# One block for the first projection, the state-space chunks and the head norm, with the units in the order u, v, q, k

## The chip, the cores and the metric

The kernel runs on one NeuronCore of one Trainium2 chip. The metric is the device time of one execution in microseconds; three runs of the kernel before took 4768.56, 4768.86 and 4769.66 us, median 4768.86. The execution that the profiler recorded took 4769.85 us, of which its span from the first to the last instruction is 4768.1 us. In what follows PE is TensorE, DVE is VectorE, ACT is ScalarE, POOL is GpSimd and SP is the queue that issues most DMAs.

## The reference, cut to what matters

The program is one block with attention, a state-space mixer, memory attention and a large expert layer, and then two more layers. Only the opening of the first block is touched:

```python
proj = _rmsnorm(h, norm_mix_g[l]) @ w_in[l]          # 512 tokens, 1024 -> 2048
q = proj[..., :512]; k = proj[..., 512:1024]          # 8 heads of 64 each
v = proj[..., 1024:1536]; u = proj[..., 1536:]
att = _chunked_attention(_rmsnorm(q, att_q_g), _rmsnorm(k, att_k_g), v, rel_bias)
ssm = _s5_mixer(u, ...)

def _s5_mixer(u, ...):                                # 32 groups of 16 channels, 64 complex states
    bu_r = einsum('blgc,gpc->blgp', uf, bbr); bu_i = einsum('blgc,gpc->blgp', uf, bbi)
    _, _, xr, xi = associative_scan(_complex_affine_combine, (a_r, a_i, bu_r, bu_i), axis=1)
    y = einsum('blgp,gcp->blgc', xr, c_re) - einsum('blgp,gcp->blgc', xi, c_im) + d_skip * uf
    ...                                               # gelu, gate, both untouched
```

## The kernel before, in words

**The projection** is one call of `project` (line 496, called at L2217). Weights come in 16 pages of 128x1024 through a ring of seven slots. ACT rounds each weight page to its high part (L190), POOL subtracts that to get the low part (L196), and PE multiplies three times for each pair of tiles: low weights by high activations, high by low, high by high. A "features" unit is one PSUM bank with 24 matmuls over 512 columns (L442, L443, L444); a "tokens" part fills four banks side by side, 12 matmuls for each of eight steps over the contraction (L616, L618, L619), so none of its four banks is complete before the end of the part. The units before are u (0 to 3), q (4 to 7), k (8 to 11) and v (the tokens part, 12 to 15). They rotate over six banks: unit n may start only after DVE has scaled unit n-6 out of its bank (semaphore `free`, L581 and L611). DVE does so at L2197 for u, at L2162 for q and k, at L2169 for v.

**The tables.** Between two such evacuations DVE works through a generator, `turn_tables` (L307, passed as `beside`), for a budget of 5.2 us by its own cost figures ahead of each features unit and 3.5 times that ahead of the first tokens unit. It makes powers of the state's decay, then 17 sets of three instructions over 128x512 (L390, L393, L396): eight for the matrices that lead into a state (`into`), nine for those that lead out of it (`outof`), then cosines and sines by doubling, and last a copy of the decay to 64 chunks (`rate`, L430). Whatever is left of the generator is run after the last budget.

**The chunks.** `state_chunks` (L1548) treats the 512 tokens as 64 chunks of 8. In a block of its own PE transposes the 32 matrices of `into` (L1595, ACT copies them out of PSUM), multiplies them with u read back through DRAM by chunks (`enter`, L1608, four batches of eight groups), and DVE turns each batch and scans it over the chunks (L1692 to L1698). The effect inside a chunk goes through eight lag kernels: 32 matmuls of 16 columns for all groups (L1652), an ACT copy, four transposes (L1659) and a spreading by DVE (L1716). Then for each batch: a matmul that swaps real and imaginary halves (`swap_ends`, L1617), DVE turns the states back (`leave`, L1707 to L1710), PE multiplies them with `outof` (L1627), ACT copies the result (L1682) and SP writes it to DRAM and reads it back in another order (L1577 to L1586), and PE adds the lags (`inside`, L1638). DVE closes each quarter with L1736.

**The head norm** (`head_norm`, L775, called at L2223) is a third block: ACT squares q and k (L802), PE sums them (L816), ACT and DVE take the root, PE spreads it (L830), DVE scales q and k (L861). After it a fourth block starts the attention.

Each `nc.Block()` ends when all engines have come to its end; the next one starts them together. Inside a block each engine runs its instructions in program order and waits on semaphores only.

## Time and profile before

| | us |
|---|---|
| median of three runs | 4768.86 |
| profiled execution | 4769.85 |
| its span | 4768.1 |
| PE busy in the span | 4498.3 (94%) |
| DVE / POOL / ACT busy | 2004.3 / 1842.5 / 1461.5 |
| first matmul of the projection | 12.72 |
| last matmul of the projection | 121.5 |
| first transpose of the chunks | 129.51 |
| last matmul of the chunks | 196.5 |
| first matmul of the head norm | 203.82 |
| first matmul of the attention | 227.75 |

The last six rows are times from the start of the span. The share of PE's busy time is an average over the whole program; what the touched stretch costs is read from its own part of the timeline. "PEclk" in a row is the share of full speed (2.4 GHz) that TensorE was granted; 0.50 is 1.2 GHz.

### The profile page before, as it was taken

To read this page: it belongs to the slowest core of one execution; us is meant where nothing else is said; L and a number is where in the kernel's file an instruction comes from. 1 tells how busy PE (TensorE), PEld (TensorE's weight loads), DVE (VectorE), ACT (ScalarE), POOL (GpSimd) and SP (SyncE) were. 2 spreads that over 40 slices of the span, in tenths; PEclk is the share of its full clock that TensorE was granted. 3 is DMA by queue.
4 is the path that set the end of the run, shared out by engine and by line. 5 is a ranking of instruction groups with operands and counts; after the bars stand their busy time and mean duration, and the time that the engine had idled before them with its cause. 6 is when DMAs were issued, how large, how long until landed. Compare 5 with 4: busy or idle time off the path is not lost. (4 is left out here: it accounts for less than half of the span.)

```text
span 4768.1 us, 51289 instructions
## 1 busy us (share of the span) xinstructions
PE 4498.3 (94%) x19930; PEld 3524.0 (74%) x19930; DVE 2004.3 (42%) x4177; ACT 1461.5 (31%) x2188; POOL 1842.5 (39%) x828
## 2 busy tenths in 40 slices
PE   7778899999999999999999979899999998788999
PEld 6557578888888888887887836588878874365887
DVE  8463369933332333333441252444144135645440
ACT  2153323344443111112222235432232232344221
POOL 3015144466665444444444401244444431032443
PEclk9789999999999999999999989999999999999999
DMA  3213134455555655654222201222222221021222
GB/s 139 45 50 111 44 102 135 139 166 177 172 183 190 196 186 184 197 184 148 93 97 94 97 16 36 67 91 95 97 89 97 95 85 51 18 76 49 97 94 83
DMA packets 220707, 520.43 MB, mean 109 GB/s; under 512 B 25649, under 2 KB 91569, under 8 KB 217521
## 3 DMA queue, kind: packets, MB, share of 16 engines
q1 hardware_dynamic: 135984, 450.03, 28.9%
q10 hardware_dynamic: 84480, 67.12, 4.3%
q8 instruction: 159, 2.61, 0.2%
q14 instruction: 84, 0.68, 0.0%
HBM read 445.77 MB, written 71.30 MB: 108 GB/s over the span
## 5 line engine op out<-in xcount | busy, mean ns | idle before, releaser
L196 POOL TENSOR_TENSOR ring_rounded<-ring,highs_rounded 128x1024 fp32r<-128x1024 f32 x687 | 1681.2, 2449 | 2644.2 <-ACT highs_rounded L190 2644.2
L442 PE MATMUL bank<-arena_rounded,ring_rounded 128*128 128x512 f32 (+1 forms) x4488 | 1778.9, 396 | 85.1 <-DVE hT_rounded L460 41.5
L444 PE MATMUL bank<-arena_rounded,highs_rounded 128*128 128x512 f32 (+1 forms) x4488 | 1757.9, 392 | 0.0
L190 ACT ACTIVATE highs_rounded<-ring 128x1024 fp32r<-128x1024 f32 x687 | 728.1, 1061 | 2039.1 <-PE bank L444 1598.5
L443 PE MATMUL bank<-hT_rounded,highs_rounded 128*128 128x512 f32 x3128 | 1221.6, 391 | 0.0
L442 PEld LDWEIGHTS bank<-arena_rounded,ring_rounded 128*128 128x128 f32 x4488 | 853.8, 190 | 271.4 <-issue 82.5
L444 PEld LDWEIGHTS bank<-arena_rounded,highs_rounded 128*128 128x128 f32 x4488 | 850.6, 190 | 193.9
L443 PE MATMUL bank<-arena_rounded,highs_rounded 128*128 128x512 f32 (+1 forms) x2112 | 824.3, 390 | 0.0
L443 PEld LDWEIGHTS bank<-hT_rounded,highs_rounded 128*128 128x128 f32 x3128 | 592.6, 189 | 125.3 <-issue 0.2
L443 PEld LDWEIGHTS bank<-arena_rounded,highs_rounded 128*128 128x128 f32 x2112 | 402.4, 191 | 86.4
L1526 DVE TENSOR_TENSOR arena<-qT,arena 128x512 f32<-128x512 f32 x64 | 149.9, 2342 | 363.6 <-ACT qT L1491 363.0
L2080 DVE TENSOR_SCALAR arena<-mats,arena 128x128 f32<-128x128 f32 x512 | 156.7, 418 | 336.8 <-PE bank L1889 336.7
L1972 ACT ACTIVATE arena<-bank 128x512 f32<-128x512 f32 x128 | 76.6, 598 | 471.5 <-PE bank L444 471.5
L438 DVE CAST arena_rounded<-arena 128x512 fp32r<-128x512 f32 x128 | 54.6, 427 | 386.6 <-PE bank L444 386.6
L442 PE MATMUL bank<-qT_rounded,ring_rounded 128*128 128x512 f32 x512 | 203.5, 397 | 0.0
L1533 DVE SCALAR_TENSOR_TENSOR xT<-bank,xT 128x512 f32<-128x512 f32 x32 | 22.1, 692 | 427.8 <-PE bank L444 427.5
L444 PE MATMUL bank<-qT_rounded,highs_rounded 128*128 128x512 f32 x512 | 200.9, 392 | 0.0
L2094 DVE TENSOR_TENSOR arena<-arena 128x512 f32<-128x512 f32 x128 | 105.8, 826 | 137.6 <-DMA arena<-gate_table 133.2
L1940 ACT ACTIVATE qT<-bank 128x512 f32<-128x512 f32 x128 | 135.0, 1138 | 22.9 <-PE bank L1889 22.9
L1889 PEld LDWEIGHTS bank<-arena 128*128 128x128 f32 x1024 | 126.0, 191 | 6.1
L1889 PE MATMUL bank<-arena 128*128 128x128 f32 x1024 | 126.4, 275 | 0.0
L1526 DVE TENSOR_TENSOR arena<-kT,arena 128x512 f32<-128x512 f32 x24 | 59.0, 2458 | 153.9 <-ACT kT L1491 153.9
(351 smaller groups left out, 4172.8 us busy)
## 6 DMA issues: line engine op xcount, KB each, us to landing
ring<-pages_in SPq DMA_DIRECT2D x687, 512.0 KB, 3.4
act_table<-arena SPq DMA_DIRECT2D x128, 256.0 KB, 4.0
gate_table<-qT SPq DMA_DIRECT2D x16, 2048.0 KB, 7.2
arena<-act_table ACTq DMA_DIRECT2D x128, 256.0 KB, 3.9
arena<-gate_table ACTq DMA_DIRECT2D x32, 1024.0 KB, 8.0
arena<-mem_in SPq DMA_DIRECT2D x3, 1024.0 KB, 5.1
arena<-spread_in SPq DMA_DIRECT2D x5, 512.0 KB, 4.4
xT<-x_in SPq DMA_DIRECT2D x8, 256.0 KB, 6.2
```

Source lines behind the costliest of these rows:

```text
L190: nc.scalar.activation(f32r(page_high(p)), slot(p), ACT.Copy).then_inc(masked_pages.sem, 1)
L196: nc.gpsimd.tensor_tensor(f32r(slot(p)), slot(p), part_of(page_high(p)), ALU.subtract).then_inc(split_pages.sem, 1)
L438: return nc.vector.tensor_copy(f32r(out), x)
L442: low_last = nc.tensor.matmul(out, f32r(w_low), f32r(x_high), start=start, stop=False)
L443: nc.tensor.matmul(out, f32r(w_high), f32r(x_low), start=False, stop=False)
L444: return low_last, nc.tensor.matmul(out, f32r(w_high), f32r(x_high), start=False, stop=stop)
L1526: nc.vector.tensor_tensor(w_low(f), w_high(f), up_scaled, ALU.mult).then_inc(made2.sem, 1)
L1889: last = nc.tensor.matmul(bank[4 + b][:, k * P:k * P + P], one1[:, b, k, :], one2[:, b, k, :], start=True, stop=True)
L1940: nc.scalar.activation(wide[:, h % 2, :, k * quad:k * quad + quad].rearrange("p j t -> p t j"), bank[4 + q % 4][:].rearrange("p (t j) -> p ...
L1972: nc.scalar.activation(kept[:, r % 2, :], bank[r % 2][:], ACT.Gelu).then_inc(made.sem, 1)
L2080: last = nc.vector.tensor_scalar(one1[:, b, k, :], iota, turnedT[:, 1, t:t + 1], turnedT[:, 0, t:t + 1], ALU.is_equal, ALU.mult)
L2094: nc.vector.tensor_tensor(raw[:, r % 3, :].rearrange("p (h t) -> p h t", h=n_half), acts_in[:, b, :].rearrange("p (h t) -> p h t", h=n_hal ...
```

## The change

1. The three blocks become one: `project`, `state_chunks` and `head_norm` take a block from outside, so that the barriers at their ends go, and waits on semaphores stand in their place.
2. The pages are laid out and the units run in the order u, v, q, k.
3. The part of u for the groups 0 to 23 is read back by chunks after weight page 15 has been asked for, into a place of its own; the part for the groups 24 to 31 after weight page 22, as the whole was before.
4. The 32 matmuls of 16 columns (L1652) are gone. The input matrices of lag 0 (`first_in`, one more set of three in the tables) are put beside the states as 16 further columns, so that the matmuls that lead out of the states take 80 columns instead of 64 and give the lag kernels too. `outof` now has eight powers (0 to 7), not nine, and `into` and `in_re` one power more each.
5. Of the sets for `outof` five stay in the tables and three are made at the start of the chunks; the copy of the decay is made for each batch.
6. The four transposes of the lags come one by one after each batch's `leave`, and `inside` runs one batch later.
7. In the chunks the banks are numbered anew (entering into 0 to 3, transposes and leaving in 4 and 5). PE's part of the head norm waits until DVE has closed the four quarters (`made2`), and the last quarter of the outputs is read back after the load of `spread`.

The diff, cut to its core:

```diff
@@ turn_tables
-            yield from turn(in_re, in_im, power_re[:, 0:8, :], power_im[:, 0:8, :], over(fr, 8), over(fi, 8), 8, groups)
+            yield from turn(in_re, in_im, power_re[:, 1:9, :], power_im[:, 1:9, :], over(fr, 8), over(fi, 8), 8, groups)
+            link(nc.vector.tensor_scalar(minus_fi, fi, gcol("sign"), -1.0, ALU.mult, ALU.mult))
...
-            for first, other, by_first, by_other, out, order in (
-                    (raw_b, other_b, in_re, in_im, into, [(7 - j, j) for j in range(8)]),
-                    (raw_c, other_c, power_re, power_im, outof, [(l, l) for l in range(9)])):
...
+            for l in range(8):
+                yield from three(raw_b, other_b, banked[0][:, l, :], banked[1][:, l, :], into[:, :, 7 - l, :])
+            yield from three(raw_b, other_b, fr, minus_fi, first_in)
             link.eng.sem_inc(tables_made.sem, 1)
...
+            for l in range(late_powers):
+                yield from three(raw_c, other_c, banked[0][:, l, :], banked[1][:, l, :], outof[:, :, l, :])
...
-            link(nc.vector.tensor_copy(rate, mag8[:, :, None].broadcast_to([P, groups, n_chunks])))
-            link(nc.vector.memset(rate[:, :, 0:1], 0.0))
-            yield 3.5
@@ state_chunks, PE
-                        if q >= 2:
-                            pe.wait_ge(turned2.sem, turned2.at(q - 1))
+                    if q < 2:
+                        pe.wait_ge(free.sem, free.at(q - 5))
+                    else:
+                        pe.wait_ge(turned2.sem, turned2.at(q - 1))
...
+                    if b >= 2:
+                        pe.wait_ge(shifted.sem, shifted.at(b - 1))
+                    else:
+                        pe.wait_ge(free.sem, free.at(2 * b - 2))
...
-                            last = nc.tensor.matmul(bank[0][:, n_chunks * g:n_chunks * g + n_chunks],
-                                                    outof[:, batch * b + g, 1:9, :].rearrange("p l c -> p (l c)"),
-                                                    before[:, batch * b + g, :], start=True, stop=True)
+                        at = wide * (g % 4)
+                        last = nc.tensor.matmul(bank[4 + g // 4][:, at:at + wide],
+                                                outof[:, batch * b + g].rearrange("p l c -> p (l c)"),
+                                                before[:, batch * b + g, :], start=True, stop=True)
...
-                    for g in range(groups):
-                        last = nc.tensor.matmul(bank[0][:, 16 * g:16 * g + 16],
-                                                outof[:, g, 0:8, :].rearrange("p l c -> p (l c)"), into[:, g, 7, :],
-                                                start=True, stop=True)
-                    last.then_inc(compared.sem, 1)
...
                     for b in range(batches):
                         leave(b)
                         if b + 2 < batches:
                             swap_ends(b + 2)
-                        inside(b)
+                    turn_lags(b)
+                    if b >= 1:
+                        inside(b - 1)
+                inside(batches - 1)
@@ state_chunks, ACT
+                    for j in range(2):
+                        last = nc.scalar.activation(
+                            lags[:, P * b + 64 * j:P * b + 64 * j + 64].rearrange("p (g c) -> p g c", g=4),
+                            left[j][:, :, n_chunks:wide], ACT.Copy)
+                    last.then_inc(drawn.sem, 1)
@@ state_chunks, DVE
+                for l in range(late_powers, chunk):
+                    link(nc.vector.tensor_tensor(q0, raw_c, over(power_re[:, l, :]), ALU.mult))
+                    link(nc.vector.tensor_tensor(q1, other_c, over(power_im[:, l, :]), ALU.mult))
+                    link(nc.vector.tensor_tensor(outof[:, :, l, :], q0, q1, ALU.add))
@@ calls
-        project(H, MH, DC, SEQ, [("features", 4, times_by_chunks), ("features", 4, times(Q)), ("features", 4, times(K)),
-                                 ("tokens", TB, times_token(lambda t: V4[:, t, :]))],
...
+        with nc.Block() as first_mixer:
+            project(H, MH, DC, SEQ, [("features", 4, times_by_chunks), ("tokens", TB, times_token(lambda t: V4[:, t, :])),
+                                     ("features", 4, times(Q)), ("features", 4, times(K))],
...
+            state_chunks(U, first_mixer)
```

Where the tokens part starts, PE's order changes as follows (L616, L618, L619 before are L623, L625, L626 after; L499 spreads the norm's root). First before, behind the last unit of k:

```order
290 L442 MATMUL bank5<-arena_rounded_54,ring_rounded_49 128x512
291 L443 MATMUL bank5<-hT_rounded_51,highs_rounded_50 128x512
292 L444 MATMUL bank5<-arena_rounded_54,highs_rounded_50 128x512
293 L616 MATMUL bank0<-ring_rounded_49,arena_rounded_54 128x512 [waits free,split_pages]
294 L618 MATMUL bank0<-highs_rounded_50,hT_rounded_51 128x512
295 L619 MATMUL bank0<-highs_rounded_50,arena_rounded_54 128x512
296 L616 MATMUL bank1<-ring_rounded_49,arena_rounded_54 128x512 [waits free]
```

And now, behind the last unit of u:

```order
99 L499 MATMUL bank6<-mats,params 128x128 [waits inverted]
100 L499 MATMUL bank6<-mats,params 128x128 x3
101 L623 MATMUL bank4<-ring_rounded_49,arena_rounded_54 128x512 [waits split_pages]
102 L625 MATMUL bank4<-highs_rounded_50,hT_rounded_51 128x512
103 L626 MATMUL bank4<-highs_rounded_50,arena_rounded_54 128x512
104 L623 MATMUL bank5<-ring_rounded_49,arena_rounded_54 128x512
105 L625 MATMUL bank5<-highs_rounded_50,hT_rounded_51 128x512
106 L626 MATMUL bank5<-highs_rounded_50,arena_rounded_54 128x512
107 L623 MATMUL bank0<-ring_rounded_49,arena_rounded_54 128x512 [waits free]
```

The part moved ahead by eight units; two of its banks are empty anyway, and the wait on `free` is now for the first and second unit of u, not for the third to sixth bank of q and k.

On PE behind the last matmul of the projection, first before (L1595 transposes, L1608 enters, L1652 makes the lags):

```order
389 L533 UNCONDITIONAL_BRANCH
390 L1588 UNCONDITIONAL_BRANCH [waits barrier_Pool_Activation_PE_DVE_SP_release]
391 L1595 MATMUL bank<-mats,arena 128x128 x8
...
410 L1608 MATMUL bank<-qT,hT 128x64 [waits shifted,turned2]
411 L1608 MATMUL bank<-qT,hT 128x64 x15
412 L1652 MATMUL bank<-arena 128x16 [waits turned2]
413 L1652 MATMUL bank<-arena 128x16 x31
414 L1617 MATMUL bank<-arena,params 128x512 [waits exped]
```

And now (L1609 transposes, L1627 enters, L1636 swaps, L1648 leaves, L1657 transposes the lags, L1665 is `inside`):

```order
389 L1600 UNCONDITIONAL_BRANCH
390 L1609 MATMUL bank<-mats,arena 128x128 [waits free]
391 L1609 MATMUL bank<-mats,arena 128x128 x3
...
413 L1627 MATMUL bank<-qT,hT 128x64 x15
414 L1636 MATMUL bank<-hT,params 128x512 [waits exped]
415 L1636 MATMUL bank<-arena,params 128x512 [waits exped]
416 L1648 MATMUL bank<-arena 128x80 [waits turned2,weighed]
417 L1648 MATMUL bank<-arena 128x80 x7
418 L1636 MATMUL bank<-arena,params 128x512 [waits weighed,exped]
419 L1657 MATMUL bank<-mats,small 128x128 [waits shifted,drawn]
```

The wait on the barrier has gone, and the matmuls of 16 columns no longer stand between entering and leaving.

On DVE, behind the tables, the order now is (L2199 evacuates k, L1759 to L1761 are the late sets, L1721 and L1723 the decay of a batch, L1725 its first instruction):

```order
222 L339 TENSOR_TENSOR qT<-bank,arena 128x16x32
223 L2199 TENSOR_TENSOR kT<-bank,small 128x512 [waits full,dve_step]
224 L2199 TENSOR_TENSOR kT<-bank,small 128x512 [waits full]
225 L1714 UNCONDITIONAL_BRANCH
226 L1759 TENSOR_TENSOR arena<-qT,arena 128x512 [waits groups_in]
...
234 L1761 TENSOR_TENSOR arena<-arena 128x32x16 [waits dve_step]
235 L1721 COPY hT<-arena 128x512 [waits dve_step]
236 L1723 MEMSET hT 128x8 [waits dve_step]
237 L1725 TENSOR_TENSOR arena<-bank,qT 128x512 [waits scored,dve_step]
```

Nine instructions over 128x512 now stand between the last evacuation and the first batch, and the table steps end before the last two units of k.

## Rows read from the trace of the kernel before

**Rows 1.** Windows by stage: us; busy PE, PEld, DVE, ACT, POOL; PEclk; DMA.
```profile
42.30:86.30 44.00, 44.00 (x195) 36.09 (x194) 42.08 (x64) 10.11 (x11) 21.59 (x9) 1.00 0.31 108
86.30:121.50 35.20, 25.16 (x97) 19.10 (x95) 31.94 (x94) 4.07 (x4) 9.90 (x4) 0.85 0.18 61
121.50:129.50 8.00, 0.02 (x1) 0.02 (x1) 7.39 (x11) 0.00 (x0) 0.00 (x0) 0.82 1.21 154
129.50:157.30 27.80, 26.42 (x161) 25.53 (x161) 9.79 (x12) 6.90 (x16) 0.00 (x0) 0.68 0.18 13
157.30:171.50 14.20, 14.20 (x74) 12.42 (x73) 5.56 (x10) 0.60 (x1) 0.00 (x0) 0.64 0.00 1
171.50:196.60 25.10, 25.02 (x133) 18.62 (x132) 12.94 (x17) 2.39 (x4) 0.00 (x0) 1.00 0.24 69
196.60:203.80 7.20, 0.00 (x0) 0.00 (x0) 2.16 (x4) 1.95 (x3) 0.00 (x0) 0.85 0.35 87
203.80:213.30 9.50, 9.44 (x16) 1.62 (x16) 0.00 (x0) 4.26 (x7) 0.00 (x0) 0.75 0.10 31
```

**Rows 2.** Timeline of PE where the tokens part waits: start, us, instruction, idle before.
```profile
99.56 0.80 PE L616 MATMUL bank<-ring_rounded,arena_rounded 128*128 128x512 f32 x1 [4.00 <-DVE kT L2162]
```

**Rows 3.** Timeline of DVE in the projection.
```profile
44.67 1.10 DVE L2197 TENSOR_TENSOR kT<-bank,small 128x512 f32<-128x512 f32 x1
50.47 1.10 DVE L2197 TENSOR_TENSOR kT<-bank,small 128x512 f32<-128x512 f32 x1
...
87.81 2.71 DVE L393 TENSOR_TENSOR arena<-qT,arena 128x512 f32<-128x512 f32 x1
90.55 0.69 DVE L396 TENSOR_TENSOR arena<-bank,arena 128x512 f32<-128x512 f32 x1
...
125.02 1.23 DVE L430 COPY arena<-arena 128x2048 f32<-128x2048 f32 x1
...
126.46 2.73 DVE L2169 TENSOR_SCALAR arena<-bank,params 128x512 f32<-128x512 f32 x4
```

**Rows 4.** Timeline of POOL at that moment.
```profile
87.26 2.71 POOL L196 TENSOR_TENSOR ring_rounded<-ring,highs_rounded 128x1024 fp32r<-128x1024 f32 x1 [3.08 <-ACT highs_rounded L190]
```

**Rows 5.** Timeline of PE in the state-space chunks.
```profile
129.51 4.01 PE L1595 MATMUL bank<-mats,arena 128*128 128x128 f32 x16 [8.00 <-PEq L533]
...
141.50 6.93 PE L1608 MATMUL bank<-qT,arena 128*128 128x64 f32 x32
...
149.93 7.50 PE L1608 MATMUL bank<-qT,hT 128*128 128x64 f32 x64
157.27 10.66 PE L1652 MATMUL bank<-arena 128*128 128x16 f32 x64
...
171.56 1.89 PE L1627 MATMUL bank<-arena 128*128 128x64 f32 x16
...
174.21 4.10 PE L1638 MATMUL bank<-kT,arena 128*128 128x512 f32 x16
```

**Rows 6.** Timeline of DVE in the chunks.
```profile
159.85 1.22 DVE L1698 TENSOR_TENSOR_SCAN hT<-arena 128x512 f32<-128x512 f32 x1
168.03 0.09 DVE L1727 MEMSET arena<- 128x32 f32 x1 [6.96 <-PE bank L1652]
...
170.66 0.68 DVE L1710 TENSOR_TENSOR arena<-arena 128x504 f32<-128x504 f32 x1
...
196.56 0.75 DVE L1736 SCALAR_TENSOR_TENSOR kT<-kT,col,bank 128x512 f32<-128x512 f32 x1 [5.04 <-PE bank L1638]
```

**Rows 7.** PE alone in windows of one us: length, busy, clock.
```profile
133.00:134.00 1.00, 0.52 (x3) 0.81 0.09 6
137.00:138.00 1.00, 1.00 (x7) 0.50 0.00 0
150.00:151.00 1.00, 1.00 (x9) 0.78 0.00 0
```

**Rows 8.** Timeline of SP's queue at the end of the chunks.
```profile
193.62 7.81 SPq L1577 DMA_DIRECT2D qT<-y_table  x16
```

More of the change, by code:

```diff
@@ L398, in turn_tables, with by_channel, three @@
-            link.eng.sem_inc(tables_made.sem, 1)
+            def by_channel(x):
+                return x[:, :, None].broadcast_to([P, groups, 16])
+            def three(first, other, by_first, by_other, out):
+                link(nc.vector.tensor_tensor(a, first, by_channel(by_first), ALU.mult))
+                yield cost(512)
+                link(nc.vector.tensor_tensor(b, other, by_channel(by_other), ALU.mult))
+                yield cost(512)
+                link(nc.vector.tensor_tensor(out, a, b, ALU.add))
+                yield cost(512)
@@ L531, in blocks @@
                     start += c
-            with nc.Block() as block:
+            with (nc.Block() if within is None else nullcontext(within)) as block:
                 @block.sync
@@ L2227, in build @@
+        for b in range(4):
+            y_kept[b].close(16)
         keep = lambda c: hT[:, c, :]
```

364 lines of the change are left out of this document (187 added, 177 removed).

## The prediction, before the change was run

> **What bounds the kernel now.** I read the page's busy shares first (PE 94% of the span), then the windows by stage, then the timelines of PE, DVE, ACT and SP in the touched stretch, and last the clock in windows of one us. The reader is to see in the windows [rows 1] that PE sets the time in all stages here, by its work or by what it waits for: it is busy throughout from 42.3 to 86.3, then 25.16 of 35.2 us while v is projected, not at all in the 8.0 us behind it, 26.42 of 27.8 us in the entering matmuls, all of the next 39.3 us, and not at all in the 7.2 us ahead of the head norm. Nothing behind the head norm is touched, and the attention waits for a block's start, so whatever the head norm's end gains or loses arrives at the end of the program. I therefore follow one chain: the projection's last matmul (121.5), the entering, the leaving, the head norm's first matmul (203.8).
>
> **1. Units in the order u, v, q, k: -4.6 us.** A features unit takes 44.0 / 8 = 5.5 us, and the 96 matmuls of the tokens part would take as much as four units, 22.0 us [rows 1]. Before they took 35.2: PE waited 10.0 us until DVE, which the tables hold up, had emptied the banks of k (the second wait is the 4.00 us of [rows 2]), and at half clock after each wait it lost the other 3.2. Now the part starts at 42.3. Its first two tiles go to banks 4 and 5, which are empty (1.4 us, to 43.7). The third needs the first unit of u gone from bank 0; DVE does that from 44.67 to 45.8 [rows 3], so PE waits 2.1. It takes 0.7, and the fourth needs the second unit, which goes at 50.47 to 51.6 [rows 3]: 5.0 us more. A restart at half clock I price at 1.5 us, half of the 3.2 that two cost before (between nothing and 3.2). Lost: 8.6 instead of 13.2. The last eight units find their banks free: DVE empties v after the large budget, at 82, and q's units at about 88, 94, 99 and 105, while the reuse by k comes at 95 to 117. So PE ends the projection at 42.3 + 22.0 + 8.6 + 44.0 = 116.9.
>
> DVE must be ready too. Its tables and evacuations run without a gap to 129.2 [rows 3]. Taken out of the projection are the set of the ninth power, 4.2 us with its long instruction (0.73, then 87.81 to 91.24), two further sets net (three late, one new) at 3 x 0.73 = 2.2 each, and the copy of the decay with its memset, 1.4; added is 0.2 for `minus_fi`: 129.2 - 4.2 - 4.4 - 1.4 + 0.2 = 119.4. That is 2.5 us behind PE. It is hidden: PE begins with transposes (4.0 us) into banks emptied earlier, and only the second batch of entering needs the last bank of k.
>
> **2. No barrier behind the projection: -8.0 us** [rows 1]. Before, PE waited for DVE's remaining tables and v's evacuation. The two bounds: the whole 8.0, or 5.5 if the 2.5 us of DVE's lag came to stand on the path. I take 8.0.
>
> **3. Transposes and entering: -1.3 us.** The 27.8 us [rows 1] had 1.4 of idle time, nearly all a wait for u read back through DRAM. Three quarters of u are now asked for after weight page 15, about 79, and have landed long before. The last quarter is asked for once weight page 15 is used up (117) and is wanted some 20 us later. Work stays the same: 16 + 32 transposes and 128 entering passes. Their price hangs on the clock: the second batch took 6.93 us at half clock, the third and fourth together 7.50 at full [rows 5, 7]. I keep the mixture of before. All at full, PE saves 6.93 - 3.75 = 3.2 and another 1.5 in the first batch, but then DVE is the bound (below); all at half costs 2 x 3.2 + 1.7 = 8 more. Entering ends at 116.9 + 26.5 = 143.4.
>
> DVE ahead of its first batch has nine instructions (6.5 us): 119.4 + 6.5 = 125.9, then the decay (1.23 / 4 + 0.15 = 0.5). PE's first batch ends at 116.9 + 4.0 + about 5 = 126. They meet, with no slack to speak of; the following batches cost DVE 3.6 + 0.5 = 4.1 us against PE's 8, so DVE catches up again. DVE's earliest end of all four is 125.9 + 4 x 4.1 = 142.3.
>
> **4. From entering to leaving: -7.0 us.** Before, PE's first leaving matmul came at 171.56, 14.3 us behind the last entering one: the lags' matmuls of 16 columns (10.66 us) stood between, and DVE sat idle 6.96 us for them [rows 5, 6]. Now DVE alone is the path: the last batch (159.85 + 1.22 - 157.27 = 3.8), its decay 0.5, the copy of `first_in` 0.7 (a 512-element instruction), the memset 0.1, and three of 0.72 = 2.2 [rows 6]: 7.3. Leaving starts at 150.7.
>
> **5. The four batches: +5.1 us.** Before they took 25.1 us at full clock [rows 1]: leaving 1.89 and lags 4.10 [rows 5] four times, two swaps. Added are: four transposes of a quarter us each (4.01 / 16), 1.0; the ACT copy between leaving and transposing (2.39 / 4 = 0.6, with its hand-overs 0.7), covered by a swap in the first two batches and open in the last two, 1.4; 80 columns instead of 64. For these the bounds are nothing (16 columns took no less each than 64 at either clock, [rows 5], so loading weights is the limit) and a quarter of 1.89 each; I take 0.3, in all 1.2. And PE now comes to this stretch from 7 us of near idleness, in which the clock falls (0.82 over the 8.0 us, [rows 1]): another restart, 1.5. Sum 5.1. The last lag matmul ends at 150.7 + 25.1 + 5.1 = 180.9.
>
> **6. No barrier ahead of the head norm: -6.2 us.** The 7.2 us before are SP's: its last 16 reads run from 193.62 to 201.43 [rows 8], then come block change, table load and squares. Now ACT has done table load and two squares by 175, and eight of the reads stand behind `spread` and beside the head norm. Left is DVE's last 0.75 [rows 6] and a hand-over, 1.0.
>
> **7. The head norm: -1.0 us.** Its 9.5 us ran at clock 0.75 [rows 1], the first half of them at 0.50. PE now comes from work at full clock. Between nothing and 2.5.
>
> Sum: -4.6 - 8.0 - 1.3 - 7.0 + 5.1 - 6.2 - 1.0 = -23.0. The profiled execution took 4769.85, 1.0 above the median of the runs shown; 4769.85 - 23.0 = 4746.9, and against the median 4745.9. I forecast 4746.
>
> **A rule against the change.** The clock came back to full while nothing but transposes had run: they begin at 129.51, and 133 to 134 has 0.81 [rows 5, 7]. The Trainium skill, TensorE: Matmul & The Clock Gate, "Part 4: PE-mode transpose", says that transposes do not count as busy for the clock and full speed "doesn't engage" for them. By it, opening the chunks with transposes would let the clock go and make the first batch all half speed, 1.7 us more in step 3; by the trace it would not. The measurement decides.
>
> **The rivals.**
>
> *A. The clock stays at half for longer, gain 8 to 18 us (chance 0.15).* For: PE was busy every microsecond from 137 to 150 and had 0.50 all the time [rows 7], so being busy with small matmuls does not buy full clock. The 8 us of step 3, and 3 or so in the batches: 4757.
>
> *B. Slower (0.05).* The same mechanism, but it holds from the projection's end to the head norm's. Step 3: +8. Batches: four times 4.1 for the lags, 1.7 for leaving, swaps 2: +25. Head norm: +4.5, transposes 1. Together 38.5 over my forecast: 4785. It comes out slower once more than 23 us are lost, so the lags' large matmuls (16.4) must be caught in it. Against: the clock was 1.00 for all 25.1 us of them before [rows 1].
>
> *C. Table work beside POOL, gain 8 to 15 us (0.08).* One table instruction took 2.71 us instead of 0.69; it reads two SBUF tiles and ran beside a POOL instruction of 2.71 us [rows 3, 4]. In the new order POOL's subtractions for q and k fall on the cosines, all through the projection. One hit costs DVE 2 us; each of ten weight pages hitting would put its end to 139, and its batches to 139 + 6.5 + 16.4 = 162 against 147.7: 14 us of the gain lost, 4760. From 86 to 126 four weight pages gave one hit, so I expect 1 to 3, which cost little: up to about 3 us DVE catches up in the entering. The Trainium skill, SBUF — State Buffer, "Who interferes with whom", says that a DVE instruction with two SBUF inputs and a GpSimd instruction that reads SBUF lock each other out, the later one for the whole length of the first. By that rule, the trace agrees.
>
> *D. More gain, 28 to 32 us (0.12).* PE never idles at the projection's end, so the clock stays up in the entering; DVE's 142.3 becomes the bound of step 3 and 4, 5 us earlier than the 147.7 above, and the restarts cost less: 4740.
>
> **How the numbers follow.** The forecast, gain 18 to 28, has 0.60: 4741 to 4751. The range for 8 of 10 takes in most of A, C and D: 4738 to 4758. Differences below 0.2% (9.5 us) cannot be told from no change. Faster by more: the forecast, D, most of A and most of C, 0.90. Within: the rest of A and C, 0.05. Slower: B, 0.05.
>
> **What would show it.** Step 1: two waits of PE of 2 and 5 us between 43 and 52, none later, last projection matmul at 117. Step 2: the first transpose within 0.3 us of it. Step 3: PE in windows of one us, entering ends by 144. Step 4: first 80-column matmul 7 us behind the last entering one, and DVE without a wait there. Step 5: 30 us from there to the last lag matmul. Step 6: first matmul of the head norm at 182, SP's reads beside it. I am wrong if PE waits for `free` or for u at the chunks' start, if DVE's late sets make the first batch wait by more than 3 us, or if the clock is at 0.50 in the lags' matmuls.

## The result

The changed kernel takes **4744.47 us** (median of 5 runs, 4741.37 to 4749.41) against 4768.86 (4768.51 to 4769.66) before: ratio 0.995, 95% interval 0.9936 to 0.9965, a gain of 24 us. The forecast was 4746. It was run twice more beside the experiments: 4744.61 (4741.77 to 4752.36) and 4746.48 (4746.12 to 4748.54). The profiled execution took 4741.37, 3 us under the median, so its rows are 28.5 us better than the profiled one of before.

### The profile page after: what moved, and what is told of

It reads as the page before. It is cut to its first block and busy times, and to the rows that moved or that the text cites. A ratio compares the mean times of both kernels' runs of the same rounds, so it can differ in the third digit from the quotient of the medians.

```text
span 4739.4 us, 51175 instructions
## 1 busy us (share of the span) xinstructions
PE 4482.7 (95%) x19866; PEld 3510.2 (74%) x19866; DVE 2017.4 (43%) x4185; ACT 1461.5 (31%) x2199; POOL 1841.9 (39%) x828
## 5 line engine op out<-in xcount | busy, mean ns | idle before, releaser
L1977 ACT ACTIVATE qT<-bank 128x512 f32<-128x512 f32 x128 | 134.9, 1136 | 22.9 <-PE bank L1926 22.9
```

The lines of the kernel that those rows point to most:

```text
L1977: nc.scalar.activation(wide[:, h % 2, :, k * quad:k * quad + quad].rearrange("p j t -> p t j"), bank[4 + q % 4][:].rearrange("p (t j) -> p ...
```

## The profile after

TensorE in the touched stretch. Columns: start, us, engine, line, operation, out<-in, shapes, count, in brackets the idle time ahead and what ended it.

```profile
45.74 0.50 PE L623 MATMUL bank<-ring_rounded,arena_rounded 128*128 128x512 f32 x1 [2.04 <-DVE kT L2234]
...
51.48 0.79 PE L623 MATMUL bank<-ring_rounded,arena_rounded 128*128 128x512 f32 x1 [4.39 <-DVE kT L2234]
...
118.04 1.03 PE L1609 MATMUL bank<-mats,arena 128*128 128x128 f32 x8
...
121.81 3.76 PE L1627 MATMUL bank<-arena 128*128 128x64 f32 x32 [0.79 <-DVE kT L2199]
...
136.72 7.04 PE L1627 MATMUL bank<-qT,hT 128*128 128x64 f32 x32
...
150.40 3.70 PE L1648 MATMUL bank<-arena 128*128 128x80 f32 x16 [3.12 <-DVEq L1743]
...
162.33 1.96 PE L1648 MATMUL bank<-arena 128*128 128x80 f32 x16
...
171.52 8.11 PE L1665 MATMUL bank<-kT,arena 128*128 128x512 f32 x32
...
180.47 7.20 PE L827 MATMUL bank<-arena,mats 128*32 128x512 f32 x16 [0.84 <-DVE kT L1775]
191.38 7.10 PE L841 MATMUL bank<-small,arena 128*128 128x512 f32 x16 [3.72 <-DVEq L866]
199.60 0.93 PE L1115 MATMUL bank<-kT,qT 64*128 64x128 f32 x8 [1.11 <-PEq L2258]
```

The 8.0 us behind the projection and the 7.2 ahead of the head norm [rows 1] are gone: the first transpose (118.04) follows the last projection matmul at once, the first entering batch then waits 0.79 us for VectorE's k tile (121.81), and the head norm starts 0.84 us behind VectorE's last lag instruction. The first 80-column matmul is at 150.40, where the 64-column one stood at 171.56 [rows 5]. The attention, which the change does not touch, starts at 199.60; before, it started here:

```profile
227.75 0.93 PE L1104 MATMUL bank<-kT,qT 64*128 64x128 f32 x8 [1.11 <-PEq L789]
```

So 28.15 of the 28.5 us are won ahead of it: 21.2 up to the leaving, less 4.1 in the four batches (29.2 us for 25.1 [rows 1]), 6.4 in the gap ahead of the head norm, 2.2 in its first projection (9.44 to 7.20), 2.5 in its second (9.66 to 7.10).

VectorE at the points that matter: one instruction of the tables that took long, the last k tiles, the first of the nine late instructions, and the first and last entering batch:

```profile
91.71 2.25 DVE L413 TENSOR_TENSOR arena<-arena 128x32 f32<-128x32 f32 x1
...
122.30 1.29 DVE L2199 TENSOR_TENSOR kT<-bank,small 128x512 f32<-128x512 f32 x2
123.50 0.68 DVE L1759 TENSOR_TENSOR arena<-qT,arena 128x512 f32<-128x512 f32 x1
...
130.63 0.69 DVE L1725 TENSOR_TENSOR arena<-bank,qT 128x512 f32<-128x512 f32 x1
...
143.87 0.69 DVE L1725 TENSOR_TENSOR arena<-bank,qT 128x512 f32<-128x512 f32 x1 [0.50 <-PE bank L1627]
```

It waits for nothing between 83 and 143.3. It is done with the projection at 123.5, where 119.4 was forecast; three instructions like L413 (0.19 us elsewhere), at 91.71, 97.66 and 103.95, took 4.5 us more than usual, and account for it. Such a long instruction is called a hit below. Each of the three ends within 0.1 us of a subtraction of GpSimd, here the first:

```profile
91.51 2.40 POOL L197 TENSOR_TENSOR ring_rounded<-ring,highs_rounded 128x1024 fp32r<-128x1024 f32 x1 [3.09 <-ACT highs_rounded L191]
```

TensorE's clock, in windows (us; busy time of PE, PEld, DVE, ACT, POOL; PEclk; DMA share, GB/s):

```profile
118.00:134.90 16.90, 14.07 (x121) 13.14 (x119) 15.81 (x27) 6.53 (x16) 0.00 (x0) 1.00 0.17 48
134.90:150.40 15.50, 12.38 (x47) 9.77 (x46) 13.43 (x21) 0.00 (x0) 0.00 (x0) 0.50 0.00 1
150.40:155.00 4.60, 4.60 (x18) 4.08 (x19) 2.05 (x3) 0.80 (x4) 0.00 (x0) 0.50 0.00 0
```

Full speed (2.4 GHz) held from 118 through all transposes and into the third entering batch; then it fell to 1.2 GHz in the middle of a batch, though TensorE was busy in every us from 134.9 to 147. The rule cited against the change (the Trainium skill, TensorE: Matmul & The Clock Gate, "Part 4: PE-mode transpose") would have had half clock here from the first transposes; by that rule, the trace does not agree. The first kernel shows it more sharply, since its clock had fallen before the transposes: it rose to 0.81 in 133 to 134 [rows 7] with nothing but transposes since 129.51.

## The experiments

"Held" is the time by which the hits (VectorE's long rows between 75 and 129) exceed their usual length. A profile has no hit, two small ones, three or five; "the pattern with three" and "with five" mean this. The columns from "held" on are of the profiled execution. e1 to e4 ran on one chip, e5 to e8 on another, e9 to e11 on a third, e12 on a fourth; each ratio is against the kernel before on the same chip.

| kernel | median (runs), us | ratio, 95% interval | held | last group of k tiles (e2, e10: of v) starts | leaving starts | attention starts | profiled |
|---|---|---|---|---|---|---|---|
| changed | 4744.47 (4741.37-4749.41) | 0.9936-0.9965 | 4.5 | 122.30 | 150.40 | 199.60 | 4741.37 |
| e1 blocks | 4749.65 (4747.52-4751.11) | 0.9947-0.9973 | 4.3 | 122.38 | 151.48 | 208.41 | 4747.52 |
| e2 order | 4739.61 (4738.12-4741.63) | 0.9925-0.9951 | 1.3 | 120.43 | 149.62 | 202.14 | 4741.63 |
| e3 before, no lag kernels | 4763.56 (4756.51-4773.03) | 0.9979-0.9996 | | | 168.85 | 229.33 | 4768.48 |
| e4 sine in PSUM | 4742.41 (4739.09-4743.22) | 0.9929-0.9955 | 4.2 | 122.97 | 150.61 | 203.43 | 4742.49 |
| e5 changed | 4744.61 (4741.77-4752.36) | 0.9936-0.9963 | 4.6 | 122.81 | 150.45 | 202.80 | 4745.68 |
| e6 no late sets | 4743.24 (4737.85-4750.42) | 0.9931-0.9958 | 9.4 | 127.57 | 155.49 | 207.79 | 4746.64 |
| e7 late on GpSimd | 4743.48 (4737.53-4744.17) | 0.9929-0.9956 | 4.2 | 122.89 | 152.29 | 205.23 | 4744.17 |
| e8 wide matmuls | 4753.25 (4737.68-4753.68) | 0.9940-0.9968 | 9.2 | 127.65 | 157.57 | 210.69 | 4753.68 |
| e9 doublings | 4741.82 (4737.77-4747.26) | 0.9923-0.9950 | 0 | 119.48 | 147.12 | 199.50 | 4741.82 |
| e10 order + e9 | 4743.48 (4740.99-4744.69) | 0.9925-0.9952 | 0 | 119.53 | 148.72 | 200.76 | 4743.48 |
| e11 changed | 4746.48 (4746.12-4748.54) | 0.9934-0.9961 | 9.3 | 127.45 | 155.30 | 207.56 | 4746.48 |
| e12 e9 + order of batches | 4736.10 (4734.68-4742.15) | 0.9921-0.9948 | 0 | 119.63 | 139.30 (next 145.27) | 196.35 | 4735.82 |

From the attention's start to the end they take 4538.9 to 4543.0 us, in two groups about 3 us apart. e5 and e11, which are the same kernel, are level until 1200 us behind the attention's start (a subtraction of GpSimd at 1201.90 and 1201.84) and 2.7 us apart at 2000 (2002.54 and 1999.86), so this comes from parts that no variant touches; its cause was not followed. The variants of the changed kernel can't be told apart by their times alone (the intervals are about 13 us wide, and all overlap that of the changed kernel); the places in the stage can.

**e1: the three blocks back**

```diff
-        with nc.Block() as first_mixer:
+        if True:
...
-                    beside=turn_tables, between_pages=rearranged, within=first_mixer)
+                    beside=turn_tables, between_pages=rearranged)
             ahead.close(16)
-            state_chunks(U, first_mixer)
+            with nc.Block() as chunks_block:
+                state_chunks(U, chunks_block)
...
```

> The changed kernel with the three blocks of before put back (order u, v, q, k and the 80-column matmuls kept). Theory (barriers are worth what PE idles at them now): the first barrier makes PE wait for DVE's last evacuation, from 118.0 to about 123.8 in the trace, +6 us; the second makes the head norm wait for block change, table load and two squares, +2.5 us: 8 to 9 us above the changed kernel, 4753. Rival 1 (the barrier's idle time also costs the clock in the entering matmuls): +12 us or more, with 0.50 from the first transpose on. Rival 2 (waits on semaphores would come to the same): +3 us or less.

Measured: 5 us above the changed kernel by medians, with overlapping intervals; its attention starts 5.6 us later than in e5. Expected were 8 to 9 us, so the theory was too high, and it lies between that and rival 2.

```profile
124.00 4.02 PE L1609 MATMUL bank<-mats,arena 128*128 128x128 f32 x16 [5.70 <-PEq L540]
...
140.20 3.74 PE L1627 MATMUL bank<-qT,hT 128*128 128x64 f32 x32
...
151.48 3.70 PE L1648 MATMUL bank<-arena 128*128 128x80 f32 x16 [5.77 <-DVEq L1743]
...
184.83 8.85 PE L827 MATMUL bank<-arena,mats 128*32 128x512 f32 x16 [3.04 <-ACT arena L811]
```

The first barrier makes TensorE idle for 5.70 us and moves the leaving by 1.1: TensorE waits for VectorE there anyway (5.77). The second costs 2.2 us of waiting and 1.65 in the head norm's first projection (8.85 for 7.20). Rival 1 fails: the clock was at 0.50 in the first transposes, but the entering batches ran at full clock (3.74 us). Together the barriers are worth 5 us beside the other parts, not the 14 of steps 2 and 6.

**e2: the order u, q, k, v**

```diff
-            project(H, MH, DC, SEQ, [("features", 4, times_by_chunks), ("tokens", TB, ...),
+            project(H, MH, DC, SEQ, [("features", 4, times_by_chunks),
                                      ("features", 4, times(Q)), ("features", 4, times(K)),
+                                     ("tokens", TB, ...)],
...
```

> The changed kernel in one block, but with the units in the order u, q, k, v as before. Theory: PE waits 10 us for k's banks as before and ends the projection at 121.3 instead of 118.0; DVE ends it at about 124 instead of 123.5, and DVE is what the entering waits for, so of the 3.3 us on PE some 1 to 3 us arrive: 4745.5 to 4747.5. Rival (the order is worth its full 4.6 us on PE, and more by the clock): +5 us or more. Rival (in this order no table step falls beside POOL's subtractions so often): 0 or a gain of up to 3 us.

Measured: no loss, where the theory had 1 to 3 us and the rival 5; the last rival (fewer hits in this order) holds. Its median is the lowest of the first four. TensorE starts its transposes at 122.25, 4.2 us later than with v second, as step 1 has it; but the leaving starts at 149.62, 0.8 earlier, since VectorE was held for 1.3 us instead of 4.5. VectorE pays for this order elsewhere, since it waits for TensorE's v unit:

```profile
120.43 2.85 DVE L2206 TENSOR_SCALAR arena<-bank,params 128x512 f32<-128x512 f32 x4 [1.17 <-PE bank L626]
```

The 4.6 us of step 1 are 4.2 on TensorE, and nothing of them arrives at the head norm (180.26 here, 180.47 and 180.98 in the changed kernel).

**e3: the kernel before with one wide matmul for the lag kernels.** It leaves the lag kernels out (one matmul of 512 columns instead of 32 of 16).

```diff
-                    for g in range(groups):
-                        last = nc.tensor.matmul(bank[0][:, 16 * g:16 * g + 16],
+                    for g in range(1):
+                        last = nc.tensor.matmul(bank[0][:],
...
```

> The kernel before, with one matmul of 512 columns in place of the 32 matmuls of 16 columns for the lag kernels (so the lag kernels are not computed, all else is). Theory (they stood alone on the path between entering and leaving): the first leaving matmul comes 7 us earlier and the program ends 7 us earlier, 4762. Rival (a restart of PE at half clock takes part of it): -5 us. Rival (DVE's work hides them): -1 us or less.

Measured: from the last entering matmul to the leaving 6.4 us (162.49 to 168.85) instead of 14.3, as step 4 has it. Its median of 12 runs is 5.8 us under before, the interval 2 to 10 us: it is faster, and the 7 us of the theory and the 5 of the first rival both lie inside. The profiled run had 3.61 us of waiting for u (1.26 in the kernel before) and more half clock in the entering, so its leaving came only 2.7 us earlier.

**e4: the sine of the doublings in PSUM**

```diff
-                for ins in (lambda: nc.vector.tensor_tensor(c2, sin, sin, ALU.mult),
-                            lambda: nc.vector.tensor_tensor(s2, sin, cos, ALU.mult),
+                for ins in (lambda: nc.vector.tensor_tensor(c2, s, sin, ALU.mult),
+                            lambda: nc.vector.tensor_tensor(s2, s, cos, ALU.mult),
```

> The changed kernel, with the doubling of sine and cosine reading one operand from PSUM instead of two from SBUF. Theory (POOL holds up table instructions that read two SBUF tiles): the three long instructions of 2.25, 1.79 and 0.99 us (0.19 otherwise) become 0.2 each, DVE ends the projection 4.5 us earlier, PE's waits of 0.8 and 1.4 us for DVE in the entering go, and 1.5 to 2.5 us arrive at the end: 4742. Rival (DVE's chain sets the whole stretch up to leaving): all 4.5 us arrive, 4740. Rival (the long instructions have another cause): they stay long and nothing changes.

Measured: L413 and L414 are at 0.19 us in all places, and the next instruction, which reads one SBUF tile and writes another, is held in their place:

```profile
92.70 0.19 DVE L413 TENSOR_TENSOR arena<-bank,arena 128x32 f32<-128x32 f32 x1
92.92 0.19 DVE L414 TENSOR_TENSOR arena<-bank,arena 128x32 f32<-128x32 f32 x1
93.15 1.93 DVE L415 TENSOR_SCALAR arena<-arena 128x32 f32<-128x32 f32 x1
```

GpSimd's instruction had started at 92.64. Nothing was gained: the wait moved on. The Trainium skill, SBUF — State Buffer, "Who interferes with whom", has instructions with two SBUF inputs contend with GpSimd, and says that `copy` and `tensor_scalar`, with one, can do so too: the traces agree, with L413 above, with this `tensor_scalar`, and with a copy in e7.

**e5: the changed kernel again**

> The changed kernel once more, beside the next three, so that their differences of a few us are read on one chip; and to see whether the second projection of the head norm (L841, 7.10 us in the trace of after, 9.85 and 9.96 us in two variants of it with the same 3.72 us of idle ahead of it) is a matter of the run. Every theory: 4744 us within 4, ratio 0.995. If the clock there is a matter of the run, L841 takes 7.1 or about 9.9 us and the first matmul of the attention (L1115) starts at 199.6 or about 202.4; if the kernel sets it, 7.1 and 199.6 again within 0.3.

Measured: L841 takes 9.79 us here, for 7.10 in the first profile, after the same 3.72 us of idle. In all other kernels here it took 9.7 to 10.1 (9.66 before), so the 7.10 was luck, 2.7 us, and it is in the 28.5 of the first profile. (In the 3.7 us of idle the granted clock stayed at 1.00 there and fell in e5, to 0.81 on average, with 0.50 behind it.) The entering ran at full clock here, and ended 3 us earlier than in the first profile:

```profile
137.02 3.76 PE L1627 MATMUL bank<-qT,hT 128*128 128x64 f32 x32 [0.50 <-DVEq L1727]
...
150.45 3.70 PE L1648 MATMUL bank<-arena 128*128 128x80 f32 x16 [7.90 <-DVEq L1743]
191.90 9.79 PE L841 MATMUL bank<-small,arena 128*128 128x512 f32 x16 [3.72 <-DVEq L866]
```

The leaving starts at the same time all the same: VectorE sets it, which waits for nothing here between its last k tile and the last batch.

**e6: without the late sets**

```diff
-                    link(nc.vector.tensor_tensor(q0, raw_c, over(power_re[:, l, :]), ALU.mult))
-                    link(nc.vector.tensor_tensor(q1, other_c, over(power_im[:, l, :]), ALU.mult))
-                    link(nc.vector.tensor_tensor(outof[:, :, l, :], q0, q1, ALU.add))
+                    link(nc.vector.memset(outof[:, :, l, :], 0.0))
```

> Leaves out part of the computation: the last three of the eight columns of the state outputs are filled with zeros instead of computed (three fills for nine VectorE instructions of 0.69 us, 6.5 us less on VectorE between 123.5 and 130.0). Theory 'VectorE sets when the states leave': its first batch starts near 125 instead of 130.63, the four batches of 4.26 us end near 143 instead of 147.4, the first matmul of the leaving starts at 145.5 to 147 instead of 150.40, and the time falls by 4 to 5 us against the changed kernel. Rival 'the half clock sets it' (TensorE at 1.2 GHz from 135 on): the entering still ends at 143.6, VectorE's fourth batch waits for it, leaving starts at 149.5 or later, and the time falls by under 1.5 us.

Measured: 1.4 us less than e5 on the same chip, within the spread. Its profile fell into another pattern, with five long instructions of 1.2 to 2.3 us on VectorE. TensorE then waits for the last k tile, and runs at half clock behind the wait:

```profile
127.09 7.06 PE L1627 MATMUL bank<-arena 128*128 128x64 f32 x32 [6.29 <-DVE kT L2197]
...
155.49 3.70 PE L1648 MATMUL bank<-arena 128*128 128x80 f32 x16 [5.56 <-DVEq L1743]
```

Its first batch waits 2.94 us for TensorE, and the leaving starts where e11, in the same pattern with the sets, has it. So the theory fails in this pattern, and the rival holds in its main point: TensorE's entering sets the leaving (it started at 127.09, behind the wait for the last k tile, and its first batch took 7.06 us at half clock). For the pattern with three no run shows it. An estimate from e5's rows: the entering ended there at 140.6 and the leaving comes 6.8 behind it, so at most 3 us could have been gained.

**e7: the late sets on GpSimd**

```diff
+                for l in range(late_powers, chunk):
+                    nc.gpsimd.tensor_tensor(outof[:, :, l, :], raw_c, many(power_re[:, l, :]), ALU.mult).then_inc(pool_step.sem, 1)
+                    nc.gpsimd.tensor_tensor(spare, other_c, many(power_im[:, l, :]), ALU.mult).then_inc(pool_step.sem, 1)
...
```

> The nine late instructions of VectorE (L1759 to L1761) run on GpSimd instead, which is idle from 115.9 on; the leaving waits for them. Theory 'moved off the path': the same gain as with them left out, 4 to 5 us; GpSimd takes 9 times about 1.2 us (half of its 2.40 us for 1024 columns) and ends near 134, long before 145. Rival 'GpSimd holds VectorE' (as in 91.71 with 2.25 us for an instruction of 0.19 beside GpSimd's 2.40): VectorE's copy, sum and scan of each batch read and write SBUF alone and would each wait up to 1.2 us while GpSimd works, so that three or four of them give 2 to 4 us back: gain 0 to 3 us, with long L1721, L1728 or L1730 rows between 123 and 136. In between I take 2.5 us.

Measured: level with e5 (0 of the 2.5 us expected), and the leaving 1.8 us later in the profile. Four of VectorE's instructions were held, 3.1 us in all, three of them here:

```profile
124.10 1.14 DVE L1743 COPY hT<-arena 128x512 f32<-128x512 f32 x1
...
128.70 1.73 DVE L1750 TENSOR_TENSOR arena<-arena 128x512 f32<-128x512 f32 x1
130.46 1.96 DVE L1752 TENSOR_TENSOR_SCAN hT<-hT,arena 128x512 f32<-128x512 f32 x1
```

(0.43, 0.69 and 1.22 usually.) The rest went to waits: VectorE now comes early and waits 1.75, 1.87 and 1.71 us for TensorE's first three batches, none of which it did in e5. TensorE's clock was at 0.50 between 126 and 137, and its second batch took 6.93 us. The account closes: 6.5 gained, less 3.1 held and 5.3 waited, is 1.9 us lost.

**e8: wide matmuls beside the entering**

```diff
+                    if b >= 1:
+                        wide_page = page_high(page.start)
+                        for j in range(6):
+                            nc.tensor.matmul(bank[6][:], f32r(wide_page[:, 0:P]), f32r(wide_page[:, 512:1024]),
+                                             start=True, stop=True)
```

> Adds six matmuls of 512 columns in fp32r behind each of the last three entering batches, into a bank that nothing reads there. At 2.4 GHz six such cost 1.3 us or more, so three groups cost 4 us of TensorE's time if nothing else changes; TensorE had waits of 1.40 and 0.79 us there and 3.12 ahead of the leaving. Theory 'the clock looks at how much flows through the array': the granted clock stays at 1.00 from 118 to 150, the batches behind 135 take 3.7 instead of 7.04 us, the leaving starts where VectorE lets it (150.0 to 150.5), the time is within 1.5 us of the changed kernel's. Rival 'the clock falls whatever flows, once there are pauses': it falls as before, near 135, and the time grows by 3 to 6 us.

Measured: the profile is in the pattern with five, so e11 is its neighbour. The three groups cost 1.63 us each and moved the leaving by 2.3. Behind the wait of 6.3 us both kernels are at half clock to about 137, and both take 3.68 us for the third batch, which is full clock, with the wide matmuls and without. They bought nothing there. But e11 shows full speed in the third and fourth batch without them, so the fall at 134.9 of the first profile, which they were to prevent, did not come up here, and the theory stands untested. Two runs of the five were at 4737.68 and 4744.24, for which there is no trace.

**e9: all doublings read PSUM**

```diff
+            d0, d1 = bank[7][:, 64:96], bank[7][:, 96:128]
+            cos_now, sin_now = bank[7][:, 0:32], bank[7][:, 32:64]
-                for ins in (lambda: nc.vector.tensor_tensor(c2, sin, sin, ALU.mult),
-                            lambda: nc.vector.tensor_tensor(s2, sin, cos, ALU.mult),
-                            lambda: nc.vector.tensor_scalar(cos, c2, -2.0, 1.0, ALU.mult, ALU.add),
-                            lambda: nc.vector.tensor_scalar(sin, s2, 2.0, None, ALU.mult)):
+                for ins in (lambda: nc.vector.tensor_tensor(d0, sin_now, sin, ALU.mult),
+                            lambda: nc.vector.tensor_tensor(d1, sin_now, cos, ALU.mult),
+                            lambda: nc.vector.tensor_scalar(cos, d0, -2.0, 1.0, ALU.mult, ALU.add),
+                            lambda: nc.vector.tensor_scalar(sin, d1, 2.0, None, ALU.mult)):
             for level in range(3):
+                link(nc.vector.tensor_copy(sin_now, sin))
                 yield from double()
...
```

> The changed kernel, in which every instruction of the angle doublings (L413 to L416) reads one operand from PSUM: the sine is copied there ahead of each of the first three (four copies of 0.20 us more), and the two intermediate products stand there. In the three traces of the changed kernel and its neighbours in which VectorE ran late, three (or, in two runs with times near 4750, five) of these instructions took 1 to 2.4 us instead of 0.19, always beside GpSimd's 2.40 us, 5.0 us or 10.4 us in all; with only the sine in PSUM (e4) the wait went over to L415, which works in SBUF alone. Theory 'instructions that work in SBUF alone are held by GpSimd, and their number in a run sets when VectorE is done': no row of L413 to L416 over 0.3 us, the last k tile is out near 119.5 instead of 123 or 127.6, the leaving starts near 146.5 instead of 150.4 or 155.5, the time is 4739 to 4741 and the spread of the runs falls under 6 us (11 for the changed kernel). Rival 'the wait goes over to the next instruction again' (the copies, L339 or the evacuations): the sum of the waits stays 5 us or more, and nothing is gained.

Measured: no long row is left between 75 and 129. The last k tiles, and the leaving:

```profile
119.48 1.29 DVE L2203 TENSOR_TENSOR kT<-bank,small 128x512 f32<-128x512 f32 x2
...
147.12 3.70 PE L1652 MATMUL bank<-arena 128*128 128x80 f32 x16 [7.82 <-DVEq L1747]
```

3.3 us ahead of e5 and e9's own neighbour e11 by 8.2. The rival (the wait goes over again) is refuted, and the leaving gains nearly all that was held: against e5 4.6 us less 0.8 for the copies is 3.8, and 3.3 arrive; against e11 it is 8.5, and 8.2 arrive. In the time it is 4.7 us below e11 on the same chip, by medians; the intervals overlap, so the gain in time isn't shown. The median is a little above the 4739 to 4741 expected, and the spread of the runs did not fall under 6 us (9.5).

**e10: both, the order and the doublings** (the edits of e2 and e9 together)

> The same with the units in the order u, q, k, v again. In e2 VectorE had two small waits (0.86 and 0.79 us), so there is 1.6 us less 0.8 us for the copies to be had by it: VectorE is done with the last v tile near 122.5 as in e2 (TensorE ends its v unit at about 122 there and sets that), late sets and batches follow: leaving starts at 149 to 149.6. Theory 'VectorE's chain alone sets the leaving': 4739 to 4741, level with e2, and here behind e9 by 2 to 3 us in the start of the leaving, since in this order the last unit ends 4 us later on TensorE. Rival 'the order is worth nothing': leaving starts within 0.5 us of e9's.

Measured: leaving at 148.72, 1.6 us behind e9's. With nothing held, the order u, v, q, k wins 1.6 us, not 4.6, nor the 2 to 3 expected, and not nothing.

**e11: the changed kernel a third time**

> The changed kernel beside them. Median 4742 to 4747, runs from 4741 to 4753. If the long instructions of VectorE between 84 and 112 come in two patterns, the profile of it shows either three (5.0 us in all, leaving at 150.4, time near 4742 to 4745) or five (10.4 us, leaving near 155.5, time 4749 to 4753).

Measured: the pattern with five, as described, two of them here:

```profile
96.78 2.32 DVE L415 TENSOR_SCALAR arena<-arena 128x32 f32<-128x32 f32 x1
102.36 2.25 DVE L413 TENSOR_TENSOR arena<-arena 128x32 f32<-128x32 f32 x1
```

Both engines are late by them. TensorE waits for the last k tile, and VectorE for TensorE only 0.3 us in all the entering, the last time at the third batch:

```profile
126.96 7.06 PE L1627 MATMUL bank<-arena 128*128 128x64 f32 x32 [6.28 <-DVE kT L2199]
...
144.52 0.69 DVE L1725 TENSOR_TENSOR arena<-bank,qT 128x512 f32<-128x512 f32 x1 [0.17 <-PE bank L1627]
```

The leaving is at 155.30, as expected. The time of that run, 4746.48, is under the expected 4749: the attention starts 4.8 us later than in e5, but this run is in the quicker of the two groups behind it.

**e12: leave early**

```diff
-                for b in range(batches):
-                    enter(b)
+                enter(0)
+                enter(1)
+                leave(0)
+                enter(2)
+                leave(1)
+                enter(3)
```

This is VectorE; TensorE follows it (leave 0, exchange 2, leave 1, two lag transposes, exchange 3, then lag groups and leaves in turn).

> The kernel of e9 with the leaving pulled ahead: on VectorE the batches go enter 0, enter 1, leave 0, enter 2, leave 1, enter 3, leave 2, leave 3 instead of four enters and four leaves, and TensorE exchanges the ends of batch 0 and 1 behind entering batches 2 and 3 and leaves batches 0 and 1 ahead of the first transposes of lags. In e9 TensorE waits 7.82 us for VectorE ahead of its first leaving at 147.12, and has 30.5 us of work from there to the last lag matmul. Theory 'TensorE's wait for VectorE can be filled': leave 0 starts near 139 and leave 1 near 145, the lag transposes near 147 (VectorE's last enter is two leaves, 4.3 us, later), TensorE's first lag group starts at 150 to 151 instead of 155.59, and has 21 us to go from there: the head norm starts at 172 to 173 instead of 177.67, the time is 4 to 5 us below e9: 4737. Rival 'the clock takes it back': with more short pauses TensorE stays at half clock until 155 or later, where each group of 16 lag matmuls takes 7 us instead of 4.11: the gain is under 2 us. Rival 'VectorE sets it anyway', since its work is the same and spread over the same span: TensorE's leave 2 and leave 3 wait for it, head norm at 176 or later.

Measured: 4736.10, the lowest median of all, 33 us under before on that chip (0.9934, interval 0.9921 to 0.9948). The changed kernel's three intervals begin at 0.9934 to 0.9936, so they overlap with this one, and by the times alone it isn't shown to be faster than that kernel; the places in the stage show it. TensorE's wait of 7.82 us is down to two of 1.81 and 0.26:

```profile
139.30 1.91 PE L1652 MATMUL bank<-arena 128*128 128x80 f32 x16
143.01 2.00 PE L1640 MATMUL bank<-arena,params 128*128 128x512 f32 x2 [1.81 <-DVEq L1739]
145.27 3.71 PE L1652 MATMUL bank<-arena 128*128 128x80 f32 x16 [0.26 <-DVEq L1751]
...
151.44 5.06 PE L1669 MATMUL bank<-kT,arena 128*128 128x512 f32 x16
...
174.48 7.20 PE L831 MATMUL bank<-arena,mats 128*32 128x512 f32 x16 [0.84 <-DVE kT L1788]
```

The head norm starts 3.2 us earlier than in e9, for 4.7 to 5.7 expected; the clock took 0.95 back in the first lag group (5.06 us for 4.11) and about 1.8 in leave 1 (3.71 for 1.96), so the second rival is right in part. Of the 6.0 us between the profiled executions of e9 and e12 only 3.15 are there at the attention's start; the rest is the two groups.

## Why the prediction was right

The time, the place of the leaving (150.40 for 150.7) and the first matmul of the head norm (180.5 for 182) came out as forecast. Its own signs of being wrong did not all stay away: TensorE did wait for a bank of k at the start of the chunks, 0.79 us here and 6.28 in e11, and that is the weak step, the end of VectorE's tables. By its steps:

1. *Order.* The waits are 2.04 and 4.39 us for 2 and 5, the projection ends at 118.0 for 116.9: the half clock behind the second wait lasted to 56.3, 4.8 us, and cost 2.4 instead of 1.5. That VectorE would be done at 119.4 failed: 123.5. The mechanism was rival C's, and 1 to 3 hits were foreseen; three cost 4.5 us and five 9.3. The lag of 2.5 us behind TensorE, "hidden", was 5.5, and it was not hidden: the first batch too waited for a bank of k, not only the second.
2. *First barrier.* 8.0 on TensorE, as forecast; undone beside the other parts it costs 1.1 at the leaving (e1). The prediction gave 5.5 as the lower bound; it should have asked what VectorE's chain is worth at the next wait.
3. *Entering.* Ends at 143.6 for 143.4, on the forecast mixture of clocks. That it came out was luck: e5 ended at 140.6, e9 at 137.4, e7 at 144.8. It mattered little: VectorE waited 0.50 us for the last batch. (There are 32 transposes before and after, not "16 + 32"; the sum doesn't use the number.)
4. *To the leaving.* 6.8 us for 7.3; e3 has 6.4 in the kernel before.
5. *Four batches.* 29.2 us for 30.2. The two copies in the open cost 0.49 each as forecast (1.4 with the hand-overs was 1.0). 80 columns cost nothing, not 0.3 each: 1.91 to 1.96 us a group, as with 64. The restart cost about 1.8 (3.70 for 1.9).
6. *Second barrier.* 6.4 for 6.2 against before. Undone (e1) it costs 2.2, and 1.65 of clock.
7. *Head norm.* 4.7 in the first profile instead of 1.0, the term most in error. 2.2 of it (7.20 for 9.44) is there in all eleven profiles without barriers, since TensorE comes from full clock; 2.5 is the luck of L841.

Why then did the sum hold? Two chains, TensorE's entering (143.6, and 6.8 behind it) and VectorE's tables, late sets and batches (123.5 + 6.5 + 4 x 4.26 + 3), meet at 150.4. The prediction followed the first and took 5 us of slack in the second ("142.3"); the hits used that slack up. Each part undone alone therefore shows less than its term (e1 5 us, e2 none): where two chains are level, the terms don't add up. With one more pair of hits both chains are late, still level to 0.3 us, and the leaving is at 155.3 (e11, and e6 with nine VectorE instructions fewer). In e5 the forecast place of the leaving (150.7) is met by the other chain: TensorE's entering ended 2.8 us before its forecast, and VectorE set the leaving at 150.45, 5 us behind its own forecast (142.3 and 3.0 more). There the agreement is luck. No run undoes two parts together or leaves out the 80-column matmuls of the changed kernel, so how the 24 us divide among the parts is argued from the rows, not shown.

## What to carry to other kernels

Work out the end of each engine's chain at each meeting point, with its own hits and clock, before terms are summed: an idle time removed on one engine is worth no more than the other engine's chain leaves free. Small VectorE instructions that stay within SBUF cost their 0.2 us only if GpSimd is quiet; beside a GpSimd instruction of 2.4 us each can cost 2.3, and giving each an operand in PSUM removed that here (the leaving came 3.3 to 8.2 us earlier; the program's time doesn't show it beyond its spread). And when an engine waits for another that works through two phases, try to interleave the phases (e12: 3.2 us at the head norm) before you shorten either.

## What was not expected of the hardware

- The hits come in patterns. Twice in three profiles of the same kernel there were three (4.5 us), once five (9.3). GpSimd's subtractions come every 5.49 us; each hit moves VectorE's next short instructions to another place in that period. What makes a run fall into one pattern or the other was not followed.
- The clock in the same small fp32 matmuls differs from run to run: the fourth entering batch took 7.04 us in the first profile and 3.76 in e5, with no more than 0.50 us of idle ahead of it in either. It stayed at 1.00 through the first 16 transposes in the changed kernel's profiles, where no barrier stood ahead of them, and it was at 0.50 to about 137 behind the waits of 6.3 us that end at 127. Behind 3.72 us of idle the next 16 matmuls took 7.10 once and 9.7 to 10.1 in the others. What decides it is not settled here, and e8 doesn't test it.
